# Feed-forward set-up of a two-block transformer kernel: earlier transposes, rows normed in two parts, full values on two engines, differences on VectorE

## The chip, the cores and the metric

The kernel runs on one core of a Trainium2 chip. The metric is the device time of one execution in microseconds (us), as the median of several runs; one more execution was profiled. Engines are TensorE (PE), VectorE (DVE), ScalarE (ACT), GpSimd (POOL) and SyncE (SP, which here only issues DMAs).

## What is computed

Two transformer blocks follow each other over 1024 tokens of width 1024, in float32. Each ends with a feed-forward layer; the second one's input is also scaled and shifted by a modulation vector:

```python
# first block
h = rmsnorm(x, g_mlp[l])
hid = jnp.square(jax.nn.relu(jnp.einsum("bsd,df->bsf", h, w_mlp_in[l])))   # 1024 -> 4096
x = x + jnp.einsum("bsf,fd->bsd", hid, w_mlp_out[l])                      # 4096 -> 1024
# second block
h = _modulate(_rmsnorm(x, g_ffn[l]), sh2, sc2)
a = jnp.square(jax.nn.relu(jnp.einsum('bsd,df->bsf', h, w_ff1[l])))
x = x + gt2[:, None, :] * jnp.einsum('bsf,fd->bsd', a, w_ff2[l])
```

## The kernel before

**Split values.** Each float32 operand x of a product is kept as a high part (a rounded copy, made on ScalarE) and a low part (x minus its high part, made on VectorE). One product then is three matmul passes: high by high, low by high, high by low.

**Seven products for eight.** The feed-forward layers multiply 2 x 2 blocks by a scheme with seven products, numbered p = 1 to 7. The weights come in 16 units u = 0 to 15 of 256 columns. For each unit the tokens' side `hq[p]` is the same, and the weights' side `wq[p]` is made anew. A product (p, u) has 12 matmuls of 128x512 (L2716 to L2718). The list `SEQ` gives the order: (1,0), (2,0), (5,0), (6,0), (7,0), (4,0), (3,0), (1,1), (2,1), and so on.

**The set-up.** Before the first product the tokens' operands have to be made. That is the stretch of this document, and it comes twice: k = 0 for the first block, k = 1 for the second. What stands in it:

- Ahead of it TensorE runs the output projection, in groups of 24 matmuls, a group for each block t = 0 to 7 of 128 tokens. VectorE adds each to the residual `xs` (L1924), and in the second block first multiplies it by a row (L2319, L2321). ScalarE squares and sums each row (`row_sum`, L1209), VectorE makes the reciprocal root (`norm_rstd`, L1534 to L1540, with one square root on ScalarE, L1214) and multiplies the rows into `xn` (L1898), t = 0 to 3 at once and t = 4 to 7 at once.
- TensorE transposes `xn` in 16 tiles n of four transposes each (L2694): n = 0 to 7 for tokens of the first half, 8 to 15 for the second. They go through four banks `XB`, so tile n waits until tile n - 4 has been read out.
- ScalarE reads each tile out as a full value `ft` ("hfull", L1230 or L1232). For n < 8 it also makes the high part (L1238) of `hq[1]` and `hq[2]`, and VectorE the low part (L1993).
- The operands of products 5, 6, 7 and 4 are differences of full values: for 5 and 6 made on VectorE (L2002, L2010), for 7 and 4 on GpSimd (L844, L850). Product 3 takes a full value as it is. Each gets a high part (ScalarE, L1251) and a low part (VectorE, L1993), in two pieces of 128x1024.
- ScalarE copies some finished banks aside (`part_kept`, L1261): product 7 may start only when the bank of product 6 has been copied, product 4 only when that of product 7 has. Product 3 waits for the sum that VectorE makes of product 7's bank (`hidden_added`, L1944).
- GpSimd makes sums and differences of each unit's weights (`unit_sums`). SP loads the raw weights of unit 1 after these operands are done, since `ft[0]` lies where unit 1 goes.

The engines' queues run in the order in which they are written; nothing is scheduled by a tool. The order on ScalarE in `ff_setup`, from the profiled kernel:

```python
for n in range(8):
    full(n)
    act.wait_ge(h_f.sem, h_f.base + 16 * k + n + 1)
    A_(hq[1 + n // 4][0][:, n % 4, :], ft[n // 4][:, n % 4, :], ACT.Copy).then_inc(h_hi.sem, 1)
for n in range(8, 16):
    full(n)
part_kept(k, 0, 0)
for p, i in ((5, 0), (6, 0), (7, 2), (4, 1), (3, 3)):
```

## Time and profile before

| | |
|---|---|
| median of 3 runs | 2657.48 us (2655.09 to 2666.38) |
| profiled execution, its own time | 2663.87 us |
| its span | 2662.0 us |
| TensorE, busy | 2490.0 us, 94% of the span |
| VectorE, busy | 1579.5 us, 59% |
| ScalarE, busy | 1207.3 us, 45% |
| GpSimd, busy | 858.9 us, 32% |

The span is what the profile shows of the execution; its own time is 1.9 us more. The first set-up lies at 889 to 944 us of the span, the second at 1994 to 2051 us. In the views a row of the timeline gives start, length, engine, line and operation, output <- inputs, how many were merged ("x4"), and in brackets how long the engine was idle before it and what released it.

### The profile page before, as it was taken

The page shows a single profiled execution, that of the slowest core. Times are in us where ns is not written, and L with a number is a line of the kernel's source. Part 1 is how long each engine was busy: PE and PEld are TensorE (multiplying, and loading weights), DVE is VectorE, ACT ScalarE, POOL GpSimd, SP SyncE. Part 2 cuts the span into 40 slices and gives each one's busy share as a digit, 9 for nine tenths or more (in the row PEclk, how much of TensorE's full clock was granted, in tenths as well). Part 3 has the DMA queues.
Part 4 walks back from the last instruction along what each step waited for, and adds up shares of the span by engine and source line. Part 5 has one row for each costly group of instructions (what it writes and reads, how often), then busy time and mean ns, then how long its engine had stood idle before and what let it go on. Part 6 is the DMA issues. An engine that isn't in the chain of part 4 may idle for free.

```text
span 2662.0 us, 32783 instructions
## 1 busy us (share of the span) xinstructions
PE 2490.0 (94%) x11852; PEld 2028.2 (76%) x11852; DVE 1579.5 (59%) x2792; ACT 1207.3 (45%) x2228; POOL 858.9 (32%) x756
## 2 busy tenths in 40 slices
PE   4997899999899899999999999999798999999997
PEld 3765778886677688887888887788686888878886
DVE  5347458988554587765545876334757444356676
ACT  6136446745412555554333453225426555543343
POOL 0222331221210166663242400005204565514242
PEclk9998999999999899999999998999998999999998
DMA  4102122323253156657754554423332444396354
GB/s 159 46 16 78 37 66 85 103 92 140 81 198 103 57 189 212 204 196 269 244 180 146 162 178 158 73 77 117 115 143 85 157 148 157 130 345 197 128 165 151
DMA packets 191187, 371.91 MB, mean 140 GB/s; under 512 B 13724, under 2 KB 58404, under 8 KB 190772
## 3 DMA queue, kind: packets, MB, share of 16 engines
q1 hardware_dynamic: 178676, 342.56, 39.0%
q10 hardware_dynamic: 8064, 14.68, 1.5%
q0 software_dynamic: 4288, 12.60, 1.5%
q8 instruction: 94, 1.54, 0.2%
q14 instruction: 65, 0.53, 0.1%
HBM read 269.05 MB, written 100.74 MB: 139 GB/s over the span
## 4 chain that ended last, share of the span: by engine, by line
PE 80%; DVE 7%; ACT 4%; DMA 3%; issue 3%; POOL 2%; SPq 0%; DVEq 0%; ACTq 0%; POOLq 0%
PE bank L2743 7%; PE bank L2745 7%; PE bank L2744 7%; PE bank L2716 7%; PE bank L2717 7%; PE bank L2718 7%; PE bank L2349 6%; PE bank L2350 6%; PE bank L2351 6%; PE bank L2530 3%; PE bank L2532 3%; PE bank L2531 3%; PE bank L2450 1%; DMA w_raw<-in_w_in 1%; PE bank L2439 1%
## 5 line engine op out<-in xcount | busy, mean ns | idle before, releaser
L2716 PE MATMUL bank<-hq_hi,wq_hi 128*128 128x512 f32 x896 | 352.3, 393 | 17.8 <-DVE hq_lo L1993 11.4
L2743 PE MATMUL bank<-ring_b_hi,ring_a_hi 128*128 128x512 f32 x896 | 350.5, 391 | 6.3 <-DVE hidden L1944 5.2
L2718 PE MATMUL bank<-hq_hi,wq_lo 128*128 128x512 f32 x896 | 350.8, 392 | 0.0
L2717 PE MATMUL bank<-hq_lo,wq_hi 128*128 128x512 f32 x896 | 350.6, 391 | 0.0
L2745 PE MATMUL bank<-ring_b_hi,ring_a_lo 128*128 128x512 f32 x896 | 349.9, 390 | 0.0
L2744 PE MATMUL bank<-ring_b_lo,ring_a_hi 128*128 128x512 f32 x896 | 349.8, 390 | 0.0
L2083 DVE TENSOR_TENSOR ring_a_lo<-a_raw,ring_a_hi 128x1024 fp32r<-128x1024 f32 x112 | 154.9, 1383 | 230.8 <-ACT ring_a_hi L1329 230.5
L1329 ACT ACTIVATE ring_a_hi<-a_raw 128x1024 fp32r<-128x1024 f32 x112 | 118.8, 1060 | 338.2 <-PE bank L2745 333.1
L1903 DVE TENSOR_TENSOR wq_lo<-unit_raw,wq_hi 128x512 fp32r<-128x512 f32 x160 | 162.5, 1020 | 110.3 <-ACT wq_hi L1195 107.3
L2716 PEld LDWEIGHTS bank<-hq_hi,wq_hi 128*128 128x128 f32 x896 | 169.3, 189 | 57.3 <-DVE hq_lo L1993 18.9
L2743 PEld LDWEIGHTS bank<-ring_b_hi,ring_a_hi 128*128 128x128 f32 x896 | 169.0, 189 | 42.9 <-DVE hidden L1944 6.1
L2718 PEld LDWEIGHTS bank<-hq_hi,wq_lo 128*128 128x128 f32 x896 | 169.3, 189 | 35.8
L2744 PEld LDWEIGHTS bank<-ring_b_lo,ring_a_hi 128*128 128x128 f32 x896 | 169.0, 189 | 35.3
L2745 PEld LDWEIGHTS bank<-ring_b_hi,ring_a_lo 128*128 128x128 f32 x896 | 168.9, 188 | 35.2
L2717 PEld LDWEIGHTS bank<-hq_lo,wq_hi 128*128 128x128 f32 x896 | 169.2, 189 | 34.7
L1195 ACT ACTIVATE wq_hi<-unit_raw 128x512 fp32r<-128x512 f32 x160 | 99.7, 627 | 142.6 <-PE bank L2718 99.0
L872 POOL TENSOR_TENSOR chain_b<-b_raw,chain_b 128x1024 f32<-128x1024 f32 x32 | 95.0, 2970 | 205.7 <-DMA b_raw<-in_w_ff 102.0
L777 POOL TENSOR_TENSOR w_lo<-w_raw,w_hi 128x512 fp32r<-128x512 f32 x56 | 75.4, 1355 | 258.1 <-ACT w_hi L966 253.7
L966 ACT ACTIVATE w_hi<-w_raw 128x512 fp32r<-128x512 f32 (+3 forms) x184 | 105.6, 605 | 104.1 <-DMA w_raw<-in_w_in 36.5
L2530 PE MATMUL bank<-hT_hi,w_hi 128*128 128x512 f32 x384 | 152.1, 396 | 0.1
L2532 PE MATMUL bank<-hT_hi,w_lo 128*128 128x512 f32 x384 | 150.3, 391 | 0.0
L2531 PE MATMUL bank<-hT_lo,w_hi 128*128 128x512 f32 x384 | 150.1, 391 | 0.0
(467 smaller groups left out, 5559.4 us busy)
## 6 DMA issues: line engine op xcount, KB each, us to landing
a_raw<-hidden_scratch SPq DMA_DIRECT2D x112, 512.0 KB, 3.3
hidden_scratch<-hidden SPq DMA_DIRECT2D x32, 1024.0 KB, 4.8
w_raw<-in_w_in SPq DMA_DIRECT2D x104, 256.0 KB, 2.8
hidden_scratch<-hidden SPq DMA_DIRECT2D x32, 768.0 KB, 3.6
unit_raw<-in_w_mlp_in SPq DMA_DIRECT2D x16, 1024.0 KB, 5.7
b_raw<-in_w_mlp_out SPq DMA_DIRECT2D x32, 512.0 KB, 4.5
unit_raw<-in_w_ff SPq DMA_DIRECT2D x16, 1024.0 KB, 5.4
b_raw<-in_w_ff SPq DMA_DIRECT2D x32, 512.0 KB, 4.6
```

What stands on the lines that cost most here:

```text
L1903: tt(wq[p][1][:, :, :], unit_operand(p, u), wq[p][0][:, :, :].bitcast(f32), ALU.subtract).then_inc(wq_lo.sem, 1)
L2349: mm(out, lh, rh, start=(i == 0), stop=False)
L2350: mm(out, lh, rl, start=False, stop=False)
L2530: mm(o[:, :], lh, rh, start=(k == 0), stop=False)
L2531: mm(o[:, :], lh, rl, start=False, stop=False)
L2532: l = mm(o[:, :], ll, rh, start=False, stop=(k == 7))
L2716: mm(o, lh[:, q, :], rh[:, q, :], start=(fresh and q == 0), stop=False, skip_group_check=True)
L2717: mm(o, lh[:, q, :], rl[:, q, :], start=False, stop=False, skip_group_check=True)
L2718: l = mm(o, ll[:, q, :], rh[:, q, :], start=False, stop=(q == 3), skip_group_check=True)
L2743: mm(o, ra_hi[r][:, e, js], rb_hi[r][:, e, :], start=(fresh and v == 0 and e == 0), stop=False, skip_group_check=True)
L2744: mm(o, ra_hi[r][:, e, js], rb_lo[r][:, e, :], start=False, stop=False, skip_group_check=True)
L2745: l = mm(o, ra_lo[r][:, e, js], rb_hi[r][:, e, :], start=False, stop=end, skip_group_check=True)
```

## The change

- **Transposes.** Tiles 0 to 3 are issued ahead of the last group (t = 7) of the output projection. Tiles 4 to 7 follow that group, then comes product (1,0), then tiles 8 to 15, then (2,0). The first two products wait for their low parts one by one.
- **Rows.** The second half is normed in two parts: rows t = 4 to 6 ahead of the last addition, and row 7 alone after it. ScalarE makes full values and high parts of tiles 0 to 3 between these.
- **Full values.** Of tiles 8 to 15 ScalarE makes the even ones and VectorE the odd ones.
- **Differences.** All four are made on VectorE, also those of products 7 and 4. GpSimd's first sums of unit 1 wait until the low part of product 4's operand is done.
- **Order.** Product (1,1) moves ahead of (6,0) (`MADE`), with its weights' split. The copy of product 6's bank comes ahead of the high parts of product 4.
- **Places.** `ft[0]` lies where unit 0's raw weights were, so SP loads unit 1 ahead of the set-up.

```diff
@@ -187,7 +187,7 @@
-        ft = [at(f"hfull{i}", [P, 4, HALF], f32, 8192 * i) for i in range(4)]
+        ft = [at(f"hfull{i}", [P, 4, HALF], f32, 8192 * i if i else RAW0) for i in range(4)]
...
@@ -353,7 +353,9 @@
-        AT = {v: i + 1 for i, v in enumerate(SEQ)}
+        MADE = SEQ[:3] + [(1, 1)] + [v for v in SEQ[3:] if v != (1, 1)]
+        AT = {v: i + 1 for i, v in enumerate(MADE)}
+        ROOT_AT = {j: j + (j > 1) + (j > 7) for j in range(10)}
...
@@ -382,7 +384,7 @@
-            return {1: (), 2: (), 5: (), 6: (), 7: (1, 2, 5, 6, 7)}.get(p, (p,))
+            return {1: (), 2: (), 5: (), 6: (), 7: (2, 5, 6, 7)}.get(p, (p,))
...
@@ -557,10 +559,10 @@
                 for t in range(NT):
                     sp.wait_ge(x_add, x0 + t + 1)
                     sp.dma_start(xr_d[k][:, t, :], xs[:, t, :]).then_inc(xr_out.sem, 16)
+                unit(1)
+                sp.wait_ge(wq_lo.sem, wq_lo.base + NP * k + WAT[3, 0])
                 sp.wait_ge(h_lo.sem, h_lo.base + 18 * k + 12)
                 sp.wait_ge(ht_p.sem, ht_p.base + 4 * k + 4)
-                unit(1)
-                sp.wait_ge(wq_lo.sem, wq_lo.base + NP * k + WAT[3, 0])
                 unit(2)
...
@@ -837,17 +839,7 @@
-                pool.wait_ge(h_f.sem, h_f.base + 16 * k + 16)
-                pool.wait_ge(ht_d.sem, ht_d.base + 4 * k + 2)
-                for r in range(2):
-                    j = slice(2 * r, 2 * r + 2)
-                    nc.gpsimd.tensor_tensor(ft[2][:, j, :], ft[3][:, j, :], ft[2][:, j, :], ALU.subtract).then_inc(ht_p.sem, 1)
-                pool.wait_ge(ht_d.sem, ht_d.base + 4 * k + 4)
-                pool.wait_ge(h_hi.sem, h_hi.base + 18 * k + 8)
-                pool.wait_ge(h_lo.sem, h_lo.base + 18 * k + 8)
-                for r in range(2):
-                    j = slice(2 * r, 2 * r + 2)
-                    nc.gpsimd.tensor_tensor(ft[1][:, j, :], ft[1][:, j, :], ft[0][:, j, :], ALU.subtract).then_inc(ht_p.sem, 1)
+                pool.wait_ge(h_lo.sem, h_lo.base + 18 * k + 16)
...
@@ -1208,43 +1200,61 @@
 
                 for t in range(4 * h, 4 * h + 4):
+                    if t == 7 and j in (1, 7):
+                        roots(ROOT_AT[j], 4, 7)
+                        act.wait_ge(wq_lo.sem, wq_lo.base + NP * (j // 7) + WAT[3, 0])
+                        first_tokens(j // 7, range(4))
                     act.wait_ge(*ready(t))
                     row_sum(j, t, junk)
-                roots(j, h)
+                if j in (1, 7):
+                    roots(ROOT_AT[j] + 1, 7, 8)
+                else:
+                    roots(ROOT_AT[j], 4 * h, 4 * h + 4)
...
+                for n in range(8, 16, 2):
+                    full(k, n)
                 part_kept(k, 0, 0)
                 for p, i in ((5, 0), (6, 0), (7, 2), (4, 1), (3, 3)):
+                    if p == 6:
+                        unit_hi(k, 1, 1)
+                    elif p == 4:
+                        part_kept(k, 0, 1)
                     for r in range(2):
                         if p in (5, 6):
-                            act.wait_ge(ht_d.sem, ht_d.base + 4 * k + 2 * (p - 5) + r + 1)
+                            act.wait_ge(ht_d.sem, ht_d.base + 8 * k + (r + 3 if p == 5 else r + 7))
                         elif p != 3:
                             act.wait_ge(ht_p.sem, ht_p.base + 4 * k + (0 if p == 7 else 2) + r + 1)
+                        else:
+                            act.wait_ge(ht_d.sem, ht_d.base + 8 * k + 6)
                         if p == 4 and r == 0:
                             act.wait_ge(xr_out.sem, xr_out.base + 128 * (k + 1))
                         j = slice(2 * r, 2 * r + 2)
...
@@ -1890,11 +1900,27 @@
-                norm_rstd(4 * h, 4 * h + 4, 2 + j)
+                norm_rstd(4 * h, 4 * h + 4, 2 + ROOT_AT[j])
+
+            def three_rows(j):
+
+                dve.wait_ge(n_ss, 10 + 4 * j + 3)
+                norm_rstd(4, 7, 2 + ROOT_AT[j])
+                normed_rows(4, 7)
+
+            def last_row(j):
+
+                dve.wait_ge(n_ss, 10 + 4 * j + 4)
+                norm_rstd(7, 8, 3 + ROOT_AT[j])
+                normed_rows(7, 8)
 
...
@@ -1907,6 +1933,17 @@
+
+            def hidden_lo(k, p, i, n, j, w):
+
+                dve.wait_ge(h_hi.sem, h_hi.base + 18 * k + n + 1)
+                tt(hq[p][1][:, j:j + w, :], ft[i][:, j:j + w, :], hq[p][0][:, j:j + w, :].bitcast(f32), ALU.subtract)\
+                    .then_inc(h_lo.sem, 1)
+
+            def first_tokens_lo(k, tiles):
+
+                for n in tiles:
+                    hidden_lo(k, 1 + n // 4, n // 4, n, n % 4, 1)
 
             for c in range(2):
                 if c == 0:
@@ -1919,6 +1956,9 @@
+                    if c == 1 and t == 7:
+                        three_rows(1)
+                        first_tokens_lo(0, range(3))
...
@@ -1928,8 +1968,8 @@
-            half_rstd(1, 1)
-            half_rows(1)
+            first_tokens_lo(0, range(3, 4))
+            last_row(1)
...
@@ -1988,34 +2028,54 @@
+                def difference(o, x, y, done):
+                    for r in range(2):
+                        j = slice(2 * r, 2 * r + 2)
+                        tt(ft[o][:, j, :], ft[x][:, j, :], ft[y][:, j, :], ALU.subtract).then_inc(done.sem, 1)
+
+                def low(p, i, n):
+                    for r in range(2):
+                        hidden_lo(k, p, i, n + r, 2 * r, 2)
+
+                def full(n):
+                    i, kk = n % 8, n % 4
+                    dve.wait_ge(f_tr.sem, f_tr.base + 16 * k + n + 1)
+                    o, x = ft[2 + i // 4][:, kk, :], XB[n % 4][:, :]
+                    if k:
+                        l = tsc(o, x, amod[:, 8 + i:9 + i], modc[:, 24 + i:25 + i], ALU.mult, ALU.add)
+                    else:
+                        l = tsc(o, x, cols[:, c_gmlp + i:c_gmlp + i + 1], None, ALU.mult)
+                    l.then_inc(ht_d.sem, 1)
+
+                first_tokens_lo(k, (4, 5))
+                full(9)
+                first_tokens_lo(k, (6,))
+                full(11)
+                first_tokens_lo(k, (7,))
                 dve.wait_ge(h_lo.sem, h_lo.base + 18 * k + 8)
-                dve.wait_ge(h_f.sem, h_f.base + 16 * k + 12)
-                for r in range(2):
-                    j = slice(2 * r, 2 * r + 2)
-                    tt(ft[0][:, j, :], ft[2][:, j, :], ft[0][:, j, :], ALU.subtract).then_inc(ht_d.sem, 1)
-                dve.wait_ge(ht_d.sem, ht_d.base + 4 * k + 2)
-                for r in range(2):
-                    low(5, 0, 8 + r, 2 * r, 2)
-                dve.wait_ge(h_f.sem, h_f.base + 16 * k + 16)
+                dve.wait_ge(h_f.sem, h_f.base + 12 * k + 10)
+                dve.wait_ge(ht_d.sem, ht_d.base + 8 * k + 2)
+                difference(0, 2, 0, ht_d)
+                full(13)
+                full(15)
+                dve.wait_ge(ht_d.sem, ht_d.base + 8 * k + 6)
+                low(5, 0, 8)
+                unit_lo(k, 1, 1)
+                dve.wait_ge(h_f.sem, h_f.base + 12 * k + 12)
                 dve.wait_ge(h_lo.sem, h_lo.base + 18 * k + 10)
-                for r in range(2):
-                    j = slice(2 * r, 2 * r + 2)
-                    tt(ft[0][:, j, :], ft[3][:, j, :], ft[0][:, j, :], ALU.subtract).then_inc(ht_d.sem, 1)
-                dve.wait_ge(ht_d.sem, ht_d.base + 4 * k + 4)
-                for r in range(2):
-                    low(6, 0, 10 + r, 2 * r, 2)
+                dve.wait_ge(ht_d.sem, ht_d.base + 8 * k + 6)
+                difference(0, 3, 0, ht_d)
+                dve.wait_ge(ht_d.sem, ht_d.base + 8 * k + 8)
+                low(6, 0, 10)
+                difference(2, 3, 2, ht_p)
                 dve.wait_ge(xr_out.sem, xr_out.base + 128 * (k + 1))
                 hidden_added(k, 0, T_A11)
-                for n, (p, i) in enumerate(((7, 2), (4, 1), (3, 3))):
-                    for r in range(2):
-                        low(p, i, 12 + 2 * n + r, 2 * r, 2)
+                dve.wait_ge(ht_p.sem, ht_p.base + 4 * k + 2)
+                low(7, 2, 12)
+                difference(1, 1, 0, ht_p)
+                dve.wait_ge(ht_p.sem, ht_p.base + 4 * k + 4)
+                low(4, 1, 14)
+                low(3, 3, 16)
 
             def sum_ready(k, o, j):
 
...
@@ -2605,6 +2668,19 @@
+
+            def hidden_transpose(k, x0, n):
+
+                if n % 8 == 0:
+                    pe.wait_ge(n_xn, x0 + n // 2 + 4)
+                if n in (13, 15):
+                    pe.wait_ge(ht_d.sem, ht_d.base + 8 * k + (n - 11) // 2)
+                elif n >= 4:
+                    pe.wait_ge(h_f.sem, h_f.base + 12 * k + (n - 3 if n < 12 else n // 2 + 3))
+                for j in range(4):
+                    l = nc.tensor.transpose(XB[n % 4][:, j * P:(j + 1) * P],
+                                            xn[:, n // 8 * 4 + j, (n % 8) * P:(n % 8 + 1) * P], ident[:, :])
+                l.then_inc(f_tr.sem, 1)
...
@@ -2658,6 +2734,9 @@
+                    if c == 1 and t == 7:
+                        for n in range(4):
+                            hidden_transpose(0, 10, n)
...
@@ -2685,20 +2764,14 @@
+                    hidden_transpose(k, x0, n)
                 pe.wait_ge(group_free, g1)
-                if k == 0:
-                    pe.wait_ge(h_f.sem, h_f.base + 16)
-                for m, (p, u) in enumerate(SEQ):
-                    if u == 0:
+                for m, (p, u) in enumerate(MADE):
+                    if u == 0 and p == 2:
+                        for n in range(8, 16):
+                            hidden_transpose(k, x0, n)
+                    if u == 0 and p > 2:
                         pe.wait_ge(h_lo.sem, h_lo.base + 18 * k + H_READY[p])
...
@@ -2713,6 +2786,8 @@
+                        if u == 0 and p <= 2:
+                            pe.wait_ge(h_lo.sem, h_lo.base + 18 * k + 4 * p - 3 + q)
...
```

Each engine's queue before and after, as built. VectorE in the first set-up, from the low parts of product 1 on (`hq1_lo`) to the sum on bank 3 (`hidden1`); before:

```order
L1993 TENSOR_TENSOR hq1_lo_208<-hfull0_221,hq1_hi_207 128x512 x4
L1993 TENSOR_TENSOR hq2_lo_210<-hfull1_222,hq2_hi_209 128x512 x4
L2002 TENSOR_TENSOR hfull0_221<-hfull2_223,hfull0_221 128x1024 x2
L1993 TENSOR_TENSOR hq5_lo_216<-hfull0_221,hq5_hi_215 128x1024 x2
L2010 TENSOR_TENSOR hfull0_221<-hfull3_224,hfull0_221 128x1024 x2
L1993 TENSOR_TENSOR hq6_lo_214<-hfull0_221,hq6_hi_213 128x1024 x2
L1944 TENSOR_TENSOR hidden1_226<-bank2,hidden1_226 128x512
L1993 TENSOR_TENSOR hq7_lo_218<-hfull2_223,hq7_hi_217 128x1024 x2
L1993 TENSOR_TENSOR hq4_lo_220<-hfull1_222,hq4_hi_219 128x1024 x2
L1993 TENSOR_TENSOR hq3_lo_212<-hfull3_224,hq3_hi_211 128x1024 x2
L1944 TENSOR_TENSOR hidden1_226<-bank3,hidden1_226 128x512
```

and now, from the low parts of product 2 on:

```order
L1940 TENSOR_TENSOR hq2_lo_210<-hfull1_222,hq2_hi_209 128x512 x2
L2047 TENSOR_SCALAR hfull2_223<-bank5,cols_55 128x512
L1940 TENSOR_TENSOR hq2_lo_210<-hfull1_222,hq2_hi_209 128x512
L2047 TENSOR_SCALAR hfull2_223<-bank7,cols_55 128x512
L1940 TENSOR_TENSOR hq2_lo_210<-hfull1_222,hq2_hi_209 128x512
L2034 TENSOR_TENSOR hfull0_221<-hfull2_223,hfull0_221 128x1024 x2
L2047 TENSOR_SCALAR hfull3_224<-bank5,cols_55 128x512
L2047 TENSOR_SCALAR hfull3_224<-bank7,cols_55 128x512
L1940 TENSOR_TENSOR hq5_lo_216<-hfull0_221,hq5_hi_215 128x1024 x2
L1929 TENSOR_TENSOR wq1_lo_190<-unit_raw1_206,wq1_hi_189 128x512
L2034 TENSOR_TENSOR hfull0_221<-hfull3_224,hfull0_221 128x1024 x2
L1940 TENSOR_TENSOR hq6_lo_214<-hfull0_221,hq6_hi_213 128x1024 x2
```

followed on the same queue by the operands of products 7, 4 and 3:

```order
L2034 TENSOR_TENSOR hfull2_223<-hfull3_224,hfull2_223 128x1024 x2
L1984 TENSOR_TENSOR hidden1_226<-bank2,hidden1_226 128x512
L1940 TENSOR_TENSOR hq7_lo_218<-hfull2_223,hq7_hi_217 128x1024 x2
L2034 TENSOR_TENSOR hfull1_222<-hfull1_222,hfull0_221 128x1024 x2
L1940 TENSOR_TENSOR hq4_lo_220<-hfull1_222,hq4_hi_219 128x1024 x2
L1940 TENSOR_TENSOR hq3_lo_212<-hfull3_224,hq3_hi_211 128x1024 x2
L1984 TENSOR_TENSOR hidden1_226<-bank3,hidden1_226 128x512
```

All four odd full values (`hfull2`, `hfull3` from bank5 and bank7) and the two pairs of differences for products 7 and 4 are new on this engine, and the low weights of (1,1) stand ahead of the second pair of differences.

ScalarE, from the last full values of the first half to the copy of product 7's bank; before:

```order
L1232 ACTIVATE hfull3_224<-bank6,cols_55 128x512
L1232 ACTIVATE hfull3_224<-bank7,cols_55 128x512
L1261 ACTIVATE hidden1_226<-bank0 128x512
L1251 ACTIVATE hq5_hi_215<-hfull0_221 128x1024 x2
L1251 ACTIVATE hq6_hi_213<-hfull0_221 128x1024 x2
L1251 ACTIVATE hq7_hi_217<-hfull2_223 128x1024 x2
L1251 ACTIVATE hq4_hi_219<-hfull1_222 128x1024 x2
L1251 ACTIVATE hq3_hi_211<-hfull3_224 128x1024 x2
L1261 ACTIVATE hidden1_226<-bank0 128x512
L1277 ACTIVATE hidden1_226<-hidden1_226 128x512
L1279 ACTIVATE hidden1_226<-hidden1_226 128x512
L1261 ACTIVATE hidden1_226<-bank0 128x512
```

and now:

```order
L1230 ACTIVATE hfull3_224<-bank6,cols_55 128x512
L1271 ACTIVATE hidden1_226<-bank0 128x512
L1261 ACTIVATE hq5_hi_215<-hfull0_221 128x1024 x2
L1187 ACTIVATE wq1_hi_189<-unit_raw1_206 128x512
L1261 ACTIVATE hq6_hi_213<-hfull0_221 128x1024 x2
L1261 ACTIVATE hq7_hi_217<-hfull2_223 128x1024 x2
L1271 ACTIVATE hidden1_226<-bank0 128x512
L1261 ACTIVATE hq4_hi_219<-hfull1_222 128x1024 x2
L1261 ACTIVATE hq3_hi_211<-hfull3_224 128x1024 x2
L1287 ACTIVATE hidden1_226<-hidden1_226 128x512
L1289 ACTIVATE hidden1_226<-hidden1_226 128x512
L1271 ACTIVATE hidden1_226<-bank0 128x512
```

The copy of bank 0 (product 6) has moved ahead of the high parts `hq4_hi`; the copy of product 7's bank still stands behind `hq3_hi` and the square of a hidden value.

## Rows read from the trace of the kernel before

**Rows 1.** Timeline of TensorE, first set-up: start, length, idle before and its releaser.

```profile
894.49 1.91 PE L2694 MATMUL bank<-ident,xn 128*128 128x128 f32 x16
...
919.14 0.50 PE L2716 MATMUL bank<-hq_hi,wq_hi 128*128 128x512 f32 x1 [1.52 <-DVE hq_lo L1993]
...
926.18 0.50 PE L2716 MATMUL bank<-hq_hi,wq_hi 128*128 128x512 f32 x1 [4.02 <-DVE hq_lo L1993]
...
930.16 0.63 PE L2718 MATMUL bank<-hq_hi,wq_lo 128*128 128x512 f32 x1
931.98 0.47 PE L2716 MATMUL bank<-hq_hi,wq_hi 128*128 128x512 f32 x1 [1.19 <-ACT hidden L1261]
...
935.72 0.47 PE L2716 MATMUL bank<-hq_hi,wq_hi 128*128 128x512 f32 x1 [0.78 <-ACT hidden L1261]
```

**Rows 2.** Timeline of TensorE, second set-up.

```profile
1999.40 1.91 PE L2694 MATMUL bank<-ident,xn 128*128 128x128 f32 x16
...
2025.92 0.50 PE L2716 MATMUL bank<-hq_hi,wq_hi 128*128 128x512 f32 x1 [3.37 <-DVE hq_lo L1993]
...
2042.54 0.47 PE L2716 MATMUL bank<-hq_hi,wq_hi 128*128 128x512 f32 x1 [0.78 <-ACT hidden L1261]
```

**Rows 3.** Stretches: busy (count) of PE, PEld, DVE, ACT, POOL; clock; DMA.

```profile
900.00:910.00 10.00, 8.85 (x35) 6.49 (x36) 6.42 (x11) 9.81 (x18) 0.00 (x0) 0.50 0.00 0
...
927.30:930.70 3.40, 3.40 (x9) 2.19 (x7) 3.40 (x3) 2.30 (x3) 1.07 (x1) 0.51 0.26 61
```

**Rows 4.** Timeline of VectorE, first set-up.

```profile
889.24 0.69 DVE L1924 TENSOR_TENSOR xs<-xs,bank 128x512 f32<-128x512 f32 x1 [0.41 <-PE bank L2351]
894.69 0.69 DVE L1924 TENSOR_TENSOR xs<-xs,bank 128x512 f32<-128x512 f32 x1 [4.76 <-PE bank L2351]
896.65 0.17 DVE L1534 TENSOR_SCALAR rst<-ss 128x4 f32<-128x4 f32 x1 [1.27 <-ACT junk L1209]
...
898.10 2.74 DVE L1898 TENSOR_SCALAR xn<-xs,rst 128x1024 f32<-128x1024 f32 x4
...
909.59 2.36 DVE L2002 TENSOR_TENSOR hfull<-hfull,hfull 128x1024 f32<-128x1024 f32 x2 [1.69 <-ACT hfull L1232]
916.59 2.49 DVE L1993 TENSOR_TENSOR hq_lo<-hfull,hq_hi 128x1024 fp32r<-128x1024 f32 x2 [4.63 <-ACT hq_hi L1251]
...
921.61 4.51 DVE L1993 TENSOR_TENSOR hq_lo<-hfull,hq_hi 128x1024 fp32r<-128x1024 f32 x2
```

**Rows 5.** Timeline of ScalarE, first set-up.

```profile
890.02 1.06 ACT L1209 ACTIVATE junk<-xs 128x1024 f32<-128x1024 f32 x1 [2.47 <-DVEq L1927]
...
898.42 0.67 ACT L1232 ACTIVATE hfull<-bank,cols 128x512 f32<-128x512 f32 x1
...
899.65 0.67 ACT L1232 ACTIVATE hfull<-bank,cols 128x512 f32<-128x512 f32 x1
...
907.08 4.71 ACT L1232 ACTIVATE hfull<-bank,cols 128x512 f32<-128x512 f32 x8
...
920.45 4.09 ACT L1251 ACTIVATE hq_hi<-hfull 128x1024 fp32r<-128x1024 f32 x4 [3.02 <-DVE hfull L2010]
...
931.26 0.58 ACT L1261 ACTIVATE hidden<-bank 128x512 f32<-128x512 f32 x1
...
932.39 0.64 ACT L1279 ACTIVATE hidden<-hidden 128x512 f32<-128x512 f32 x1
```

**Rows 6.** Timeline of GpSimd, first set-up.

```profile
921.63 6.74 POOL L850 TENSOR_TENSOR hfull<-hfull,hfull 128x1024 f32<-128x1024 f32 x2 [4.76 <-DVE hfull L2010]
933.88 2.39 POOL L813 TENSOR_TENSOR wsum<-unit_raw 128x512 f32<-128x512 f32 x1 [5.51 <-DMA unit_raw<-in_w_mlp_in]
...
938.20 1.62 POOL L817 TENSOR_TENSOR wsum<-unit_raw 128x512 f32<-128x512 f32 x1
```

**Rows 7.** Groups of VectorE by form: a tensor-scalar that reads PSUM, busy and mean ns.

```profile
L2119 DVE TENSOR_SCALAR bank<-bank,amod,modc 128x512 f32<-128x512 f32 x8 | 6.5, 813 | 6.3 <-PE bank L2374 6.3
```

**Rows 8.** Timeline of ScalarE, second set-up: one full value.

```profile
2004.09 0.76 ACT L1230 ACTIVATE hfull<-bank,modc,amod 128x512 f32<-128x512 f32 x1
```

77 lines of the change are left out of this document (34 added, 43 removed).

## Prediction

> **What bounds the kernel now.** TensorE does: it is busy for 2490.0 of 2662.0 us. So I read its timeline in the two set-ups first, since an engine that is busy elsewhere can gain only where it waits. In the first set-up the reader sees the last group end at 894.49, where the transposes start, and then waits ahead of products: 1.52 for (5,0) and 4.02 for (6,0), for low parts from VectorE, and 1.19 and 0.78 for (7,0) and (4,0), for copies of banks by ScalarE [rows 1]. From (4,0) at 935.72 on there is no more wait. (4,0), (3,0) and (1,1) have 36 matmuls; a matmul takes 0.227 us there, as the last group of 24 before the set-up took 5.45 us between two additions [rows 4]. So (2,1) starts at 935.72 + 8.17 = 943.9. That start is my measure, since ahead of it the same work stands in both kernels. In the second set-up it is 2042.54 + 8.17 = 2050.7 [rows 2].
>
> Second, the clock. In the stretch 900 to 910 it was granted at 0.50 (1.2 of 2.4 GHz), with transposes alone on TensorE, and at 0.51 in 927.3 to 930.7, after the 4.02 wait [rows 3]. There product (6,0) took 926.18 to about 930.6, 4.4 us, where 12 matmuls at 0.227 take 2.7: 1.7 lost [rows 1].
>
> Third, VectorE and ScalarE, for what the waits are made of [rows 4, 5], and GpSimd [rows 6]. A pair of 128x1024 low parts took 2.49 us on VectorE with GpSimd silent (at 916.59), and 4.51 beside GpSimd's subtractions (at 921.61), and those took 3.37 each.
>
> **The new chain, first set-up.** Its times are worked out from these rows, on the time scale of before; a released engine starts 0.05 to 0.2 us after its releaser, as in the rows.
>
> The last group started at 894.49 - 5.44 = 889.05. Now 16 transposes of 1.91 us [rows 1] stand ahead of it, so it ends at 896.4. They cost nothing: they stood behind it before. ScalarE ends row 6's sum at 891.2 [rows 5]. The root takes 1.45 (896.65 to 898.10) and a row 0.69 (2.74 for four) [rows 4], so three rows are normed at 894.8. ScalarE makes a full value and its high part per 1.23 us (898.42 to 899.65) [rows 5], four from 891.9 to 896.8. Three low parts of 0.62 end at 896.7, then comes the addition of t = 7, to 897.4, row 7's sum, to 898.7, its root and its row, to 900.9. That is no earlier than the 900.84 of before [rows 4]. What is new is what TensorE does meanwhile: tiles 4 to 7 and all of (1,0), done at 896.4 + 1.9 + 2.7 = 901.0.
>
> Tiles 8 to 11 follow ScalarE's full values 4 to 7, one per 1.23 from 899.4 on, to 904.3; even full values then take 0.59 (4.71 for eight) [rows 5]. The last transpose ends at about 907.1 and (2,0) at 909.8. Odd full values on VectorE have no row. Below stands an addition that reads PSUM, 0.69 [rows 4], above a tensor-scalar that reads and writes PSUM, 0.81 [rows 7]; I take 0.72, since the new one reads PSUM but writes SBUF. The ends are 0.5 us apart for four.
>
> From here VectorE sets the pace. Low part 7 ends at 905.95, the pair of differences for (5,0) at 908.3 (2.36 a pair [rows 4]), two full values at 909.75, the pair of low parts at 912.25. So (5,0) starts at 912.3. The low weights of (1,1) take 0.6, and (1,1) follows at once, to 917.75. The pair for (6,0) is made in 2.36 + 2.49: (6,0) starts at 917.8. A pair of differences, the sum on product 2's bank (0.63) and a pair of low parts make 5.5: (7,0) starts at 923.3. GpSimd is silent in all this, so I take the 2.49, not the 4.51. Differences and low parts for (4,0) end at 928.1.
>
> But (4,0) also waits for the copy of product 7's bank. On ScalarE this stands behind the second high part of (4,0), which ends at 926.7, two high parts of (3,0) at 1.02 (4.09 for four), a square in two steps, 1.25, and itself, 0.52 [rows 5]: 930.5. **(4,0) starts at 930.5**, after a wait of 4.5 us. Now GpSimd starts its sums of unit 1, at 928.2, so the two low parts of (3,0) take the contended 2.25 each: to 932.6. The sum on product 7's bank ends at 933.2, (3,0) starts at 933.3 and **(2,1) at 936.0**, against 943.9: 7.9 us earlier.
>
> A rule of the Trainium skill gives another price here. In "SBUF — State Buffer", section "Who interferes with whom", a VectorE instruction with two SBUF inputs and a GpSimd instruction that reads SBUF exclude each other, and the loser waits for the whole of the other. By it the two low parts of (3,0) would each wait for a GpSimd sum. The trace does not bear out the whole waits: the pair at 921.61 took 4.51 beside a subtraction of 3.37 [rows 4, 6], where one such wait alone would make 2.49 + 3.37 = 5.9. By the rule, two waits of 1.7 for GpSimd's sums would make 5.9 of the 4.5 in the chain, and (3,0) 1.4 later; in the forecast below that would be hidden behind (4,0). I go by the row.
>
> **The clock's share.** The 4.5 us wait ahead of (4,0) is as long as the 4.02 that cost 1.7 in (6,0) [rows 1, 3]. I charge it: (4,0) then ends at 934.9 and (3,0) starts there, 1.6 later. In the transposes of the second half the clock may also fall, as it did at 900; they then need about 2 us more, of which VectorE's chain hides more than half. I charge 0.4. Gain: 7.9 - 1.6 - 0.4 = 5.9 us.
>
> **Second set-up.** There the addition takes two instructions and a full value 0.76 instead of 0.67 [rows 8], both in both kernels: over one more instruction of 0.7, eight full values at 0.09 and four at 0.1 the new chain is 1.8 us longer, 48.8 instead of 47.0 from the group's start. That start is 1999.40 - 5.44 = 1993.96 [rows 2], so (2,1) would start at 2042.7, 8.0 earlier. Less 1.6, and less 0.7 since the slower tiles leave TensorE idler: 5.7.
>
> **What it costs elsewhere.** Four full values (2.9 us) and four differences (4.7) move to VectorE, two of them from GpSimd; they are in the chain above. Unit 1's load moves ahead of everything: SP issues it behind the eighth residual store, at about 898, and the load takes about 5.5: before, it was issued when GpSimd's last subtraction ended (921.63 + 6.74 = 928.37), and GpSimd then waited 5.51 for it [rows 6]. So it is there at about 904, and (1,1) needs its high weights only at 912. Behind ScalarE's late copy stand four weights, two squares and two weights of unit 1, then the copy of (1,1)'s bank, for which (6,1) waits. GpSimd's sums took 2.39 and then 1.7 (the third starts at 938.20 and takes 1.62 [rows 6]); from 928.2 on the last ends at about 934.1. Two more weights, the squares (2.5), two weights and the copy (0.5 each) follow: 939.3. (6,1) would start at 938.7 without the clock's loss, and at 940.3 with it. So the copy fits in the forecast with 1.0 to spare, and would be 0.6 late without the clock's loss.
>
> **Sum.** 5.9 + 5.7 = 11.6 us. The profiled execution's own 2663.87 would become 2652.3. It lies 6.4 above the median of the runs, 2657.48; against that I expect **2646**, 0.43% less. A measurement of this kernel tells a change from none at about 0.5%, 13.3 us, a time of 2644.2.
>
> **Rivals.** *The clock holds, 32%.* If the wait ahead of (4,0) costs nothing, or falls where the loss is hidden, (6,1) waits 0.6 for its copy, and the gain is 7.3 + 7.4 = 14.7: 2642.8. For it: the wait of 1.52 at 919.14 was followed by full clock, (6,0) began at full clock after its 4.02, and 1.6 of loss in (4,0) has 0.6 hidden already. Against it: each wait of 3.3 or more here was followed by a product partly at half clock.
>
> *The gain is given back, 13%.* The spare of 1.0 at (6,1) is small, and past it each us is lost in full. If all three of GpSimd's sums take 2.39, as the one at 933.88 [rows 6], and the weights' low parts on VectorE come late enough to hold GpSimd and ScalarE up once more, the copy ends at about 943: 3 us per set-up are lost, 2652. For it: three engines meet there in 10 us. Against it: in the trace before the same work ran after (7,0) with no wait on TensorE from 935.72 on.
>
> *VectorE is dearer than alone, 5%, and slower than before.* Between 906 and 928 stand 16 instructions of 128x1024 on it, priced at 1.2. If what slowed the pair at 921.61 was not GpSimd but ScalarE's high parts, they cost 2.25: 16 us later in each set-up, 8 net of the gain: 2657.5 + 16 = 2674. From 0.5 us each on no gain is left, from 0.9 on it is slower by over 0.5%. Against it: at 916.59 a pair took 2.49 right behind a high part, with ScalarE otherwise idle, so the row excludes it only in part.
>
> **Chances and range.** Forecast 50%, with a range of its own of 2644.2 to 2649. Faster by over 0.5% is the clock's rival, 0.32. Within 0.5%: forecast and given back, 0.63. Slower by over 0.5%: 0.05. The range for 8 in 10 reaches from the clock's rival with 0.69 us full values and the runs' own scatter, 2639, through the given-back case at 2652 to 2654, and leaves out the dear VectorE.
>
> **What would show it.** Right: (1,0) done ahead of tile 8; (5,0) 23.2 us after the last group's transposes began, (6,0) 5.5 behind it, (7,0) another 5.5; the wait of 4.5 at (4,0) released by ScalarE's copy; pairs at 2.4 to 2.5 on VectorE; (2,1) 47 to 49 us behind them. Wrong: odd full values over 0.81, a wait at (6,1), pairs over 3 us while GpSimd is silent, or clock losses in other places.

## The result

The changed kernel runs in 2647.5 us, median of 7 runs (2642.37 to 2650.2), against 2657.68 for the kernel before in the same comparison: ratio 0.9949, 95% interval 0.9936 to 0.9962. A second comparison gave 2643.6 against 2659.07, ratio 0.9946 (0.9932 to 0.9959). So it gains about 14 us, 0.5%. Forecast were 11.6 us and a time of 2646. The two gains lie just past the 0.5% that I had drawn as the line between faster and no change.

The profiled execution took 2647.55 us (2663.87 before). The page after:

```profile
span 2645.8 us, 32798 instructions
PE 2481.8 (94%) x11852; PEld 2024.3 (77%) x11852; DVE 1590.5 (60%) x2820; ACT 1203.4 (45%) x2222; POOL 837.6 (32%) x748
L2791 PE MATMUL bank<-hq_hi,wq_hi 128*128 128x512 f32 x896 | 352.9, 394 | 15.0 <-ACT hidden L1271 8.3
L2792 PE MATMUL bank<-hq_lo,wq_hi 128*128 128x512 f32 x896 | 350.6, 391 | 0.0
```

VectorE's busy time rose by 11.0 us and GpSimd's fell by 21.3. The product's matmuls are now L2791 to L2793; what they still wait for is ScalarE's copies.

TensorE's timeline in the first set-up, with start, length and the wait before, against [rows 1]:

```profile
887.11 1.91 PE L2681 MATMUL bank<-ident,xn 128*128 128x128 f32 x16
...
894.33 1.91 PE L2681 MATMUL bank<-ident,xn 128*128 128x128 f32 x16
...
902.67 1.97 PE L2681 MATMUL bank<-ident,xn 128*128 128x128 f32 x16 [0.58 <-ACT hfull L1230]
...
909.65 0.50 PE L2791 MATMUL bank<-hq_hi,wq_hi 128*128 128x512 f32 x1 [2.26 <-DVE hq_lo L1940]
...
920.51 0.47 PE L2791 MATMUL bank<-hq_hi,wq_hi 128*128 128x512 f32 x1 [0.78 <-ACT hidden L1271]
...
927.09 0.47 PE L2791 MATMUL bank<-hq_hi,wq_hi 128*128 128x512 f32 x1 [3.57 <-ACT hidden L1271]
...
930.13 0.63 PE L2791 MATMUL bank<-hq_hi,wq_hi 128*128 128x512 f32 x1
931.41 0.49 PE L2791 MATMUL bank<-hq_hi,wq_hi 128*128 128x512 f32 x1
...
934.25 0.39 PE L2791 MATMUL bank<-hq_hi,wq_hi 128*128 128x512 f32 x1
```

The reader sees the forecast's shape. The first 16 transposes stand ahead of the last group. (1,0) starts at 896.00 and is done ahead of tile 8. The 4.02 wait of (6,0) is gone, and the long wait is now at (4,0), for ScalarE's copy. (3,0) starts at 931.41 and (2,1) at 934.25.

The measure is the start of (2,1) from the place of the last group. That place starts at 887.11 here, with the transposes now ahead of the group, and it started at 889.05 before. The second set-up's place is 1985.97, and its (2,1) starts at 2034.65:

| start, from the place of the last group | forecast | first set-up | second set-up |
|---|---|---|---|
| (5,0) | 23.25 | 22.54 | 24.25 |
| (6,0) | 28.75 | 29.74 | 29.82 |
| (7,0) | 34.25 | 33.40 | 34.69 |
| (4,0) | 41.45 | 39.98 | 41.70 |
| (2,1), second set-up's forecast 51.1 | 48.95 | 47.14 | 48.68 |
| (2,1) before | | 54.95 | 56.86 |

The forecast for the first set-up is the prediction's, less 889.05, with its 2.0 of clock loss in the last line but one; the second's is its 48.8 with 2.3. So the gains are 7.8 and 8.2, in sum 16.0 of the 16.2 by which the span is shorter. (6,1), next behind (2,1), starts 2.72 later in both and waits for nothing.

VectorE's timeline of the first set-up, against [rows 4]:

```profile
900.21 0.75 DVE L2047 TENSOR_SCALAR hfull<-bank,cols 128x512 f32<-128x512 f32 x1
...
903.51 2.36 DVE L2034 TENSOR_TENSOR hfull<-hfull,hfull 128x1024 f32<-128x1024 f32 x2
905.79 1.41 DVE L2047 TENSOR_SCALAR hfull<-bank,cols 128x512 f32<-128x512 f32 x2
907.23 2.36 DVE L1940 TENSOR_TENSOR hq_lo<-hfull,hq_hi 128x1024 fp32r<-128x1024 f32 x2
909.51 0.68 DVE L1929 TENSOR_TENSOR wq_lo<-unit_raw,wq_hi 128x512 fp32r<-128x512 f32 x1
...
919.94 2.35 DVE L2034 TENSOR_TENSOR hfull<-hfull,hfull 128x1024 f32<-128x1024 f32 x2
922.35 5.70 DVE L1940 TENSOR_TENSOR hq_lo<-hfull,hq_hi 128x1024 fp32r<-128x1024 f32 x4
927.98 0.68 DVE L1984 TENSOR_TENSOR hidden<-bank,hidden 128x512 f32<-128x512 f32 x1
```

From 903.51 to 927.98 it has no gap of note. A pair has a length of 2.36, but the next instruction starts 2.28 after the pair's start (907.23 to 909.51). In 5.70 for four, the last pair is 5.70 - 2.28 = 3.4, not 4.5.

ScalarE and GpSimd where (4,0) waits, and where the copy for (6,1) is made:

```profile
921.19 4.08 ACT L1261 ACTIVATE hq_hi<-hfull 128x1024 fp32r<-128x1024 f32 x4 [0.82 <-DVE hfull L2034]
...
926.37 0.58 ACT L1271 ACTIVATE hidden<-bank 128x512 f32<-128x512 f32 x1
...
935.36 0.58 ACT L1271 ACTIVATE part<-bank 128x512 f32<-128x512 f32 x1
```

```profile
924.79 2.18 POOL L815 TENSOR_TENSOR wsum<-unit_raw 128x512 f32<-128x512 f32 x1 [69.12 <-DVE hq_lo L1940]
```

The copy of (1,1)'s bank ends at 935.94, and (6,1) starts at 936.97: 1.0 to spare, as the forecast had it.

Stretches of the first set-up (busy time and count of each engine, then the clock), against [rows 3]:

```profile
900.00:910.00 10.00, 6.38 (x38) 5.03 (x39) 9.36 (x12) 7.42 (x12) 0.00 (x0) 1.00 0.09 32
911.00:914.40 3.40, 3.40 (x10) 2.67 (x9) 3.34 (x4) 2.11 (x2) 0.00 (x0) 0.52 0.00 0
928.10:931.50 3.40, 3.40 (x10) 2.63 (x9) 3.20 (x3) 1.21 (x3) 3.24 (x3) 0.51 0.07 24
```

900 to 910 is at full clock now. Two pieces of 3.4 us are at 1.2 GHz: one in (5,0) and (1,1), one in (4,0), which takes 931.41 - 927.09 = 4.3 us where the next takes 2.84. In the second set-up one piece lies in the transposes of the second half instead (0.50 in 2004 to 2006), and one again in (4,0), which takes 4.24.

### The profile page after: what moved, and what is told of

It reads as the page before. It is cut to its first block, busy times and chain, and to the rows that moved or that the text cites. A ratio compares the mean times of both kernels' runs of the same rounds, so it can differ in the third digit from the quotient of the medians.

```text
span 2645.8 us, 32798 instructions
## 1 busy us (share of the span) xinstructions
PE 2481.8 (94%) x11852; PEld 2024.3 (77%) x11852; DVE 1590.5 (60%) x2820; ACT 1203.4 (45%) x2222; POOL 837.6 (32%) x748
## 4 chain that ended last, share of the span: by engine, by line
PE 56%; DVE 5%; ACT 2%; DMA 2%; POOL 1%; issue 1%; SPq 0%; DVEq 0%; ACTq 0%; POOLq 0%
PE bank L2818 7%; PE bank L2820 7%; PE bank L2819 7%; PE bank L2791 7%; PE bank L2793 7%; PE bank L2792 7%; PE bank L2412 3%; PE bank L2413 3%; PE bank L2414 3%; DMA w_raw<-in_w_in 1%; PE bank L2977 1%; DVE hfull L2034 1%; DVE ring_b_lo L2146 1%; DVE hq_lo L1940 1%; PE bank L2968 0%
## 5 line engine op out<-in xcount | busy, mean ns | idle before, releaser
L2791 PE MATMUL bank<-hq_hi,wq_hi 128*128 128x512 f32 x896 | 352.9, 394 | 15.0 <-ACT hidden L1271 8.3
L2793 PE MATMUL bank<-hq_hi,wq_lo 128*128 128x512 f32 x896 | 350.5, 391 | 0.0
L2791 PEld LDWEIGHTS bank<-hq_hi,wq_hi 128*128 128x128 f32 x896 | 169.4, 189 | 53.5 <-DVE hq_lo L1940 11.9
L2793 PEld LDWEIGHTS bank<-hq_hi,wq_lo 128*128 128x128 f32 x896 | 169.3, 189 | 35.7
```

The lines of the kernel that those rows point to most:

```text
L2791: mm(o, lh[:, q, :], rh[:, q, :], start=(fresh and q == 0), stop=False, skip_group_check=True)
L2793: l = mm(o, ll[:, q, :], rh[:, q, :], start=False, stop=(q == 3), skip_group_check=True)
```

## The experiments

All are compared by the start of (6,1) from the last group's place, since some of them add a wait there. Ratios are to the kernel before, with 95% intervals. Beside (1,1) behind (3,0), GpSimd's sums early, the first run of the filled gap and product 7's copy early, the kernel before had a median of 2659.05; beside the other parts undone 2658.43; beside the repeats, the early rows alone and the last kernel 2659.07.

| kernel | median us | ratio | (6,1), first | (6,1), second |
|---|---|---|---|---|
| before | 2657.68 | | 57.67 | 59.58 |
| changed kernel | 2647.5 | 0.9949 (0.9936 to 0.9962) | 49.86 | 51.40 |
| the same again | 2643.6 | 0.9946 (0.9932 to 0.9959) | 49.88 | 51.38 |
| no early rows or transposes | 2652.14 | 0.9976 (0.9966 to 0.9986) | 54.79 | 55.33 |
| two differences on GpSimd | 2649.01 | 0.9970 (0.9957 to 0.9982) | 54.68 | 54.46 |
| copy of product 6's bank late | 2649.66 | 0.9969 (0.9960 to 0.9979) | 53.02 | 54.47 |
| (1,1) behind (3,0) | 2649.36 | 0.9966 (0.9955 to 0.9976) | 51.99 | 53.89 |
| full values all on ScalarE | 2649.08 | 0.9947 (0.9931 to 0.9963) | 51.67 | 52.74 |
| early rows and transposes alone | 2654.87 | 0.9980 (0.9969 to 0.9990) | 55.88 | 57.57 |
| GpSimd's sums early | 2649.10 | 0.9970 (0.9960 to 0.9980) | 52.91 | 56.31 |
| gap ahead of (4,0) filled | 2638.66 | 0.9929 (0.9909 to 0.9949) | 49.00 | 50.89 |
| the same again | 2642.3 | 0.9938 (0.9925 to 0.9952) | 49.45 | 50.87 |
| product 7's copy early | 2641.88 | 0.9937 (0.9915 to 0.9959) | 50.75 | 50.51 |
| copies early, two gaps filled | 2640.57 | 0.9933 (0.9920 to 0.9946) | 47.93 | 50.33 |

The two right-hand columns come from one profiled execution each. In the changed kernel's two they agree within 0.02 us, in the filled kernel's within 0.45. By the intervals of the ratios alone, only the kernel without early rows and transposes, and the one with them alone, are clear of the changed kernel in both its comparisons; for the other parts the cost rests on the profiles.

**The changed kernel again.** No edit.

> The changed kernel once more, in the same batch as three others, for a closer figure of what it gains. Its profiled execution was 16.2 us shorter than that of before, and 15.9 of it lies in the two set-ups, while the first comparison gave a ratio of 0.9949 and medians 10.2 us apart. Theory: the set-ups are worth about 16 us less about 2 by chance in the clock elsewhere, ratio 0.994 to 0.996. Rival: part of the gain is given back where the profile did not show it, ratio 0.997 or nearer to 1.

The set-ups came out within 0.03 us of the first profile, and the ratio was 0.9946. Nothing shows that the set-ups' gain is given back later; the interval still leaves room for about 5 us.

### One part undone

**No early rows or transposes.** The second half is normed after the last addition and all transposes follow the last group; the rest is as changed.

```diff
-                    if c == 1 and t == 7:
-                        for n in range(4):
-                            hidden_transpose(0, 10, n)
...
-                for n in range(4, 8):
+                for n in range(8):
                     hidden_transpose(k, x0, n)
```

> The changed kernel without the early transposes and without the norm in two parts: eight tiles follow row 7, as before the change. My chain: the rows are complete at the same time, but ScalarE and VectorE then have four tiles more to do behind them, 4 x 1.23 = 4.9 us on ScalarE; (5,0) and all after it, (2,1) too, 3.5 to 4.5 us later in each set-up, 7 to 9 us in all. Rival (the rows' end sets it, so the early tiles hide nothing): within 1 us.

Undone, it costs 4.9 and 3.9 us, the first more than expected: (4,0) also took 5.08 there, against 4.32. This is the largest part by the sum of both.

**Two differences on GpSimd.** Those of products 7 and 4 go back; GpSimd's sums still wait for the low parts of (4,0).

```diff
+                    nc.gpsimd.tensor_tensor(ft[2][:, j, :], ft[3][:, j, :], ft[2][:, j, :], ALU.subtract).then_inc(ht_p.sem, 1)
...
+                    nc.gpsimd.tensor_tensor(ft[1][:, j, :], ft[1][:, j, :], ft[0][:, j, :], ALU.subtract).then_inc(ht_p.sem, 1)
...
-                difference(2, 3, 2, ht_p)
...
-                difference(1, 1, 0, ht_p)
```

> The changed kernel with the differences of products 7 and 4 back on GpSimd. My theory (GpSimd's reads slow VectorE, not ScalarE's copies): VectorE saves 4.7 us of its own, but its pairs beside GpSimd take 4 to 4.6 us instead of 2.3, and low part of (4,0) ends 1 to 4 us later; (2,1) 1 to 3 us later in each set-up, 2 to 6 us in all. Rival (VectorE is the pace, so any work off it helps): pairs stay at 2.3, (2,1) 2 to 4 us earlier.

It costs 4.8 and 3.1 us, more than expected. VectorE and GpSimd in its first set-up:

```profile
905.82 4.50 DVE L1951 TENSOR_TENSOR hq_lo<-hfull,hq_hi 128x1024 fp32r<-128x1024 f32 x2
910.25 2.85 DVE L1940 TENSOR_TENSOR wq_lo<-unit_raw,wq_hi 128x512 fp32r<-128x512 f32 x1
...
915.42 4.56 DVE L1951 TENSOR_TENSOR hq_lo<-hfull,hq_hi 128x1024 fp32r<-128x1024 f32 x2
...
920.50 3.94 DVE L1951 TENSOR_TENSOR hq_lo<-hfull,hq_hi 128x1024 fp32r<-128x1024 f32 x2
```

```profile
905.93 6.61 POOL L846 TENSOR_TENSOR hfull<-hfull,hfull 128x1024 f32<-128x1024 f32 x2 [51.65 <-DVE hfull L2058]
915.44 6.79 POOL L852 TENSOR_TENSOR hfull<-hfull,hfull 128x1024 f32<-128x1024 f32 x2 [2.90 <-DVE hfull L2045]
```

VectorE has two pairs fewer, which saves it 4.6 us. But the three pairs of low parts beside GpSimd take 4.50, 4.56 and 3.94 instead of 2.36 each, and the low weights of (1,1) 2.85 instead of 0.68: 8.1 us more. So GpSimd costs VectorE more than it takes off it, and (7,0) and (4,0) depend on its 6.6 and 6.8 us besides.

The rows also show what one such wait is. The first two subtractions end at 909.24 and 912.54. The low weights stand listed from 910.25 to 913.09, so they end 0.55 behind the second subtraction: they waited until it was done.

**Copy of product 6's bank late.** It goes back behind all high parts.

```diff
-                    elif p == 4:
-                        part_kept(k, 0, 1)
...
-                    elif p == 6 and u:
+                    elif p == 6:
                         part_kept(k, u, 1)
```

> The changed kernel with one part undone: the copy of product 6's bank is back behind the high parts of (4,0) and (3,0). My chain: (7,0) then starts after that copy, about 5.3 us later than in the changed kernel, with a wait of about 6 us on ScalarE; the copy of product 7's bank follows, so (4,0) starts 2.3 us later, and (2,1) 0.5 to 2.3 later (47.1 and 48.7 us after the slot of the last group become 47.6 to 51). Rival (the order of copies does nothing, since (4,0) waits for ScalarE anyway): (2,1) within 0.5 us. Whole kernel: 1 to 5 us slower than the changed one by my chain, 0 by the rival.

TensorE in its first set-up; the edit moves a ScalarE copy, and this row names VectorE:

```profile
921.50 0.76 PE L2789 MATMUL bank<-hq_hi,wq_hi 128*128 128x512 f32 x1 [7.77 <-DVE hq_lo L1938]
927.38 0.47 PE L2789 MATMUL bank<-hq_hi,wq_hi 128*128 128x512 f32 x1 [0.78 <-ACT hidden L1269]
```

```profile
920.78 0.57 ACT L1269 ACTIVATE hidden<-bank 128x512 f32<-128x512 f32 x1
```

(7,0) waits 7.77 us instead of 0.78. The copy ends at 921.35 and (7,0) starts at 921.50, while its low parts had been ready since 915.6. So the wait ends with the copy, though the row puts it down to VectorE; in the second set-up the same wait, 6.18, is put down to ScalarE's copy. (4,0) then waits 0.78 instead of 3.57, and 3.2 and 3.1 us are the net cost, where 0.5 to 2.3 were expected. The half-clock loss moves with the long wait: here it is in (7,0), which takes 927.38 - 921.50 - 0.78 = 5.1 us.

**(1,1) behind (3,0).** The order of before, and its weights' split with it.

```diff
-        MADE = SEQ[:3] + [(1, 1)] + [v for v in SEQ[3:] if v != (1, 1)]
+        MADE = list(SEQ)
...
-                    if p == 6:
-                        unit_hi(k, 1, 1)
...
-                unit_lo(k, 1, 1)
```

> The changed kernel with product (1,1) back in its old place behind (3,0), its weights' split with it. My chain: nothing fills the time between (5,0) and (6,0), which VectorE sets; (6,0), (7,0) and (4,0) start 0.6 us earlier (low weights gone from VectorE), the 2.7 us of (1,1) come at the end: (2,1) 2.1 us later, up to 3.7 if the longer wait lowers the clock. 4 to 7 us in all. Rival (the order costs nothing as ScalarE and VectorE are the pace to the end): within 0.5 us.

It costs 2.1 and 2.5 us. TensorE then waits in four places of the first set-up, 2.24, 1.82, 2.12 and 2.47; in the changed kernel it is three, 2.26, 0.78 and 3.57, so (1,1) fills 2.0 us of waits, as work that depends on nothing late. No wait here is longer than 2.5 us, and yet (4,0), behind the last of four, took 4.28 and 4.25 us at a mean clock of 0.63. So the half-clock loss doesn't need a wait of 3.6 us or more; several shorter ones in a row brought it too.

**Full values all on ScalarE.**

```diff
-                for n in range(8, 16, 2):
+                for n in range(8, 16):
                     full(k, n)
...
-                full(9)
...
-                full(11)
...
-                full(13)
-                full(15)
...
```

> The changed kernel with all full values back on ScalarE. My chain: ScalarE ends them 1.9 us later, so the high part of (5,0) and with it VectorE's low parts start about 1.1 us later, although VectorE has 2.9 us less to do; (5,0) to (4,0) and (2,1) 0.5 to 1.5 us later, 1 to 3 us in all. Rival (VectorE alone is the pace): (5,0) about 1 to 2 us earlier, 2 to 4 us faster in all.

By the set-ups it costs 1.8 and 1.3 us. The runs don't show it: four are 2641.6, 2642.73, 2649.08 and 2659.27. A fifth, of 14068 us, is an outlier that the table's median, 2649.08, counts and the ratio does not; without it the median is 2645.9. The profiled one has a span of 2657.5 with a mean clock of 0.975. The difference in span to the changed kernel's, 11.7, is mostly not in the set-ups; the last section comes back to it.

The undone parts add up to 16.8 and 13.9 us, where the whole change brings 7.8 and 8.2. So the parts don't add. A likely reason is that the set-up is one chain through three engines, where any part taken out can become the slowest piece. The next run shows it for one part; the others were not tried by themselves.

**Early rows and transposes alone.** The kernel before with that part, with (1,0) ahead of tiles 8 to 15, and with unit 1's load ahead. No other part.

> Of the change only the early part: three rows normed ahead, four tiles transposed ahead of the last group, (1,0) ahead of tiles 8 to 15, and unit 1's load ahead. Full values on ScalarE, two pairs of differences on GpSimd, (1,1) behind (3,0) and the copies in their old places. Undoing this part alone cost 4.9 and 3.9 us. Theory that the parts cover one another (one chain over three engines, where the slowest piece left decides): alone it brings less than that, about 2.8 us, (2,1) 52 us from the group's start instead of 55.0, ratio 0.998. Rival, that the parts add: 4.9 and 3.9 us, (2,1) at 50 and 53, ratio 0.9965.

It brings 1.8 and 2.0 us, where undoing the same part cost 4.9 and 3.9. About 2.8 were expected. VectorE shows where the rest of the gain went:

```profile
908.69 5.30 DVE L1944 TENSOR_TENSOR hq_lo<-hfull,hq_hi 128x1024 fp32r<-128x1024 f32 x2 [1.61 <-ACT hq_hi L1265]
...
921.58 11.72 DVE L1944 TENSOR_TENSOR hq_lo<-hfull,hq_hi 128x1024 fp32r<-128x1024 f32 x6
```

(7,0) was still 3.4 us earlier than before (39.54 against 42.93 from the place). But GpSimd's subtractions lie beside two pairs again, and with unit 1 loaded early its sums start at 923.26 and lie beside the last ones: six low parts take 11.72, 1.95 each, against 8.48 in the kernel before. So part of the loss here is the early load's and not the rows'. How much of it reached TensorE, I can't tell from this run; no run has the early load alone.

### The prices in dispute

**GpSimd's sums early.** They wait for the low parts of (5,0) instead of those of (4,0).

```diff
-                pool.wait_ge(h_lo.sem, h_lo.base + 18 * k + 16)
+                pool.wait_ge(h_lo.sem, h_lo.base + 18 * k + 10)
```

> The changed kernel with GpSimd's first sums of unit 1 let go once the low part of (5,0) is done, not that of (4,0). Theory (GpSimd's reads slow VectorE): three sums of about 2.2 us run beside the differences and low parts of (6,0) and (7,0); a pair there takes 3.5 to 4.6 us instead of 2.3, (6,0) starts about 2 to 3 us later, (2,1) 1 to 2.5 later: 2 to 5 us slower in all. Rival (what slows VectorE is ScalarE): pairs stay at 2.3, (6,0) in place, and with the weights ready earlier (2,1) is up to 1 us earlier.

```profile
908.75 4.53 DVE L2034 TENSOR_TENSOR hfull<-hfull,hfull 128x1024 f32<-128x1024 f32 x2
913.32 3.34 DVE L1940 TENSOR_TENSOR hq_lo<-hfull,hq_hi 128x1024 fp32r<-128x1024 f32 x2
916.59 2.35 DVE L2034 TENSOR_TENSOR hfull<-hfull,hfull 128x1024 f32<-128x1024 f32 x2
```

```profile
908.32 1.66 POOL L815 TENSOR_TENSOR wsum<-unit_raw 128x512 f32<-128x512 f32 x1 [53.99 <-DVE hq_lo L1940]
910.06 2.15 POOL L817 TENSOR_TENSOR unit_raw<-unit_raw 128x512 f32<-128x512 f32 x1
912.28 2.16 POOL L819 TENSOR_TENSOR wsum<-unit_raw 128x512 f32<-128x512 f32 x1
```

The first set-up is 3.0 longer, the second 4.9, where 1 to 2.5 each were expected; in the second (4,0) and (3,0) also took 5.25 and 3.20, at a mean clock of 0.64. Three sums of 6.0 us in all make two VectorE pairs 3.2 us longer, 2.2 and 1.0. The same pair takes 2.35 as soon as GpSimd is silent. So 1.2 for a VectorE instruction alone was right, and the difference comes from GpSimd. ScalarE's high parts ran beside VectorE's cheap pairs in every one of these traces, and the rival "VectorE is dearer than alone" falls with that.

The Trainium skill has a rule for this, in "SBUF — State Buffer", section "Who interferes with whom": the two engines exclude each other and the loser waits for the whole of the other's instruction. The trace agrees. The sums end at 909.98, 912.21 and 914.44, and a VectorE instruction ends 1.1 behind each, at 911.06, 913.29 and 915.53; 1.1 is the distance of two such instructions when VectorE is alone. The three waits cost 3.2 and not 6.0 because the listed lengths of the sums hold their own waits for VectorE: a sum beside an idle VectorE takes 1.3 (933.16 to 934.46 in this run), the later two of these 2.15. It is the same with GpSimd's subtractions in the kernel before. In turn with VectorE they took 3.37 each [rows 6], and beside a VectorE idle until 916.59 they took 2.4 each:

```profile
912.10 4.77 POOL L844 TENSOR_TENSOR hfull<-hfull,hfull 128x1024 f32<-128x1024 f32 x2 [54.49 <-DVE hfull L2002]
```

**The gap ahead of (4,0) filled.** Twelve matmuls on ready tiles, into a bank that nobody reads.

```diff
+                    if (p, u) == (4, 0):
+                        pe.wait_ge(wq_lo.sem, wq_lo.base + NP * k + WAT[4, 0])
+                        for q in range(12):
+                            mm(XB[3][:, :], wq[4][0][:, q % 4, :], hq[7][0][:, q % 4, :], start=(q == 0), stop=(q == 11),
+                               skip_group_check=True)
```

> The changed kernel with 12 added matmuls (their result is never read) between (7,0) and (4,0), 2.7 us in a wait of 3.6 and 4.0. Theory (the wait lowers the clock): no 0.5 clock at (4,0), its 12 matmuls take 2.7 to 3.0 instead of 4.2, (2,1) 1.2 to 1.6 us earlier in each set-up; of that up to 0.5 is lost again at (6,1), whose bank copy comes then. 1.5 to 3 us faster in all. Rival (the clock's fall is not from this wait): (4,0) still takes 4.2 and nothing is gained, or the added work comes in the way and costs up to 1 us.

```profile
921.89 2.88 PE L2777 MATMUL bank<-hq_hi,wq_hi 128*128 128x512 f32 x12
926.01 0.47 PE L2796 MATMUL bank<-hq_hi,wq_hi 128*128 128x512 f32 x1 [1.24 <-ACT hidden L1271]
...
928.82 0.39 PE L2796 MATMUL bank<-hq_hi,wq_hi 128*128 128x512 f32 x1
...
935.02 0.47 PE L2796 MATMUL bank<-hq_hi,wq_hi 128*128 128x512 f32 x1 [0.61 <-ACT part L1271]
```

The stretch of (4,0) in this kernel, and one that is mostly (3,0):

```profile
926.00:929.50 3.50, 3.49 (x16) 2.91 (x17) 3.35 (x4) 1.02 (x2) 3.42 (x2) 1.00 0.34 129
928.10:931.50 3.40, 3.40 (x16) 2.81 (x15) 3.10 (x3) 2.27 (x4) 3.24 (x3) 1.00 0.00 0
```

(4,0) starts at the same distance from the place, 39.99 against 39.98, and takes 2.81 us at full clock instead of 4.32. The first wait after (4,0) is then at (6,1), 0.61 us, for the copy of (1,1)'s bank: what the forecast's first rival said, and of its size in the first set-up (0.93 in the second). Net of it 0.9 and 0.5 us are kept. The ratio was 0.0020, or 5 us, below the changed kernel's, which the set-ups do not explain. The same kernel again:

> The twelve idle-time matmuls ahead of (4,0) once more (they multiply ready tiles into a bank that nobody reads; the sums are as before). By the first trace the product (4,0) then runs at full clock and (2,1) starts 1.6 us earlier in each set-up, of which (6,1) keeps 0.9 and 0.5, since it then waits for the copy of (1,1)'s bank. Theory: it is worth about 1.4 us against the changed kernel, and the 5 us by which the first comparison had it faster was chance in the clock elsewhere. Rival: the full clock carries on beyond the set-up, and it is worth 4 to 6 us.

Beside the changed kernel it was 1.3 us faster by the medians, 0.4 and 0.5 by the set-ups, with intervals that overlap. The rest of the first figure did not come again, so I take it for scatter.

### Towards a better version

**Product 7's copy early.** Ahead of the high parts of (3,0), with the sum on that bank ahead of the low parts of (3,0).

```diff
+                    elif p == 3:
+                        part_kept(k, 0, 2)
...
                 low(4, 1, 14)
+                hidden_added(k, 0, T_A22)
                 low(3, 3, 16)
```

> The changed kernel with the copy of product 7's bank ahead of the high parts of (3,0) on ScalarE, and the sum on that bank ahead of the low parts of (3,0) on VectorE. My chain: (4,0) starts 2.4 us earlier, when its low part is done, (3,0) and (2,1) 3.3 us earlier; but (6,1) then waits about 2.3 us for the copy of (1,1)'s bank, which ends as late as before, so about 1 us is kept in each set-up: 2 us faster in all. Rival (no other wait behind it): 3.3 us kept in each, 6.6 in all.

```profile
927.61 0.47 PE L2794 MATMUL bank<-hq_hi,wq_hi 128*128 128x512 f32 x1 [0.78 <-ACT hidden L1273]
932.95 0.80 PE L2794 MATMUL bank<-hq_hi,wq_hi 128*128 128x512 f32 x1 [2.35 <-DVE hq_lo L1942]
```

```profile
928.45 4.44 DVE L1942 TENSOR_TENSOR hq_lo<-hfull,hq_hi 128x1024 fp32r<-128x1024 f32 x2 [0.19 <-ACT hq_hi L1263]
```

(4,0) starts 1.5 earlier from the place (38.43), but (3,0) now waits 2.35, for low parts that start later and both lie beside GpSimd's sums, 4.44 for the pair. Behind that wait (3,0) took 4.26 us. In the first set-up this loses 0.9 and in the second it gains 0.9, where 1 us kept in each was expected: the wait, and in the first set-up the clock's loss, went from one product to the next. The median, 2641.88 of 4 runs, is no evidence for more.

**Copies early, two gaps filled.** In addition the copy of (1,1)'s bank goes directly behind the high parts of (2,1), and 8 and 6 idle matmuls stand ahead of (4,0) and (3,0).

```diff
                             unit_hi(k, p_, u + 1)
+                            if (p_, u) == (2, 0):
+                                act.wait_ge(h_lo.sem, h_lo.base + 18 * k + 18)
+                                part_kept(k, 1, 0)
...
+                    if u == 0 and p in (4, 3):
+                        pe.wait_ge(wq_lo.sem, wq_lo.base + NP * k + WAT[p, 0])
+                        for q in range(8 if p == 4 else 6):
+                            mm(XB[3][:, :], wq[p][0][:, q % 4, :], hq[7][0][:, q % 4, :], start=(q == 0),
+                               stop=(q == (7 if p == 4 else 5)), skip_group_check=True)
```

> Copy of product 7's bank ahead of the high parts of (3,0), the copy of (1,1)'s bank behind the high parts of (2,1), and idle-time matmuls in the gaps: 8 ahead of (4,0), 6 ahead of (3,0). With the early copy alone (4,0) started 38.4 and 39.5 us from the group's start instead of 40.0 and 41.7, (3,0) waited 2.35 and 1.67 for its low parts, and part of (3,0) was at half clock. Theory: with the gaps filled (2,1) starts at 46.5 and 46.0 instead of 47.1 and 48.7, (6,1) at 49.3 and 48.8 instead of 49.9 and 51.4, so about 3 us less than the changed kernel, and half-clock periods in the set-ups are fewer. Rival: VectorE has become the bound there, and the filled gaps only move the waits: no gain over the changed kernel.

```profile
900.00:935.00 35.00, 29.29 (x136) 23.09 (x136) 33.61 (x32) 23.81 (x35) 8.43 (x5) 1.00 0.17 55
```

The first set-up is at full clock, and VectorE is busy for 33.61 of these 35 us. The second is not: 2000 to 2012 has 0.86. (6,1) starts 1.9 and 1.1 earlier than in the changed kernel, 3.0 in sum as expected, though the expectation had 0.6 and 2.6. The medians of the same comparison are 3.0 apart. The intervals of the two ratios overlap. So this version has the shortest set-ups and the lowest median of its comparison, but the runs alone don't show it to be the fastest; the filled kernel's first median, in another comparison, was 2638.66.

## Why the prediction was right, and where it was off

- **Early transposes, three rows, (1,0) ahead of tile 8.** As forecast, to the order: low part 7 ended at 903.5, 16.4 us from the place, forecast 16.9. The run without early rows and transposes puts 4.9 and 3.9 us on these. (1,0) stayed ahead of tile 8 in it, and no run moved it back.
- **VectorE sets the pace.** Right, and its odd full values took 0.746 and, in the second set-up, 0.806 each, inside the bounds of 0.69 and 0.81. **The term that was mis-sized is the pair.** I took 2.36 and 2.49, the listed lengths in [rows 4]. What counts on a busy engine is the distance of starts, 2.28. Seven pairs stand ahead of the differences' end for (4,0): 16.0 us instead of 16.9. With the 0.5 ahead of them that is the 1.5 us by which (4,0) came earlier than forecast. It is most of the 1.8 and 2.4 us by which each set-up beat its sum; 0.5 more of the second's is its clock charge, below.
- **The contended pair of (3,0), and the rule that I set aside.** Charged 4.5, it took 3.4. It was hidden behind (4,0) either way. The 2.25 for each low part was an average over a pair that did not behave evenly, and the reading behind it was wrong. At 921.61 in the kernel before, the first low part took 1.23 as if alone, and the second was listed at 3.37 and ended at 926.12, 1.08 behind the end of GpSimd's first subtraction. That is one wait for a whole subtraction. I held 2.49 + 3.37 = 5.9 against it, but the subtraction's 3.4 holds its own wait for VectorE. Beside an idle VectorE a subtraction takes 2.4, as shown under the early sums. So the row agrees with the rule of the Trainium skill ("SBUF — State Buffer", section "Who interferes with whom"). It is chance that 2.25 was also right beside sums: there each low part waits 1.1, in the pair of 921.61 one of two waits 2.2. In the changed kernel the first low part of (3,0) began at 924.63, ahead of the sum, and only the second waited: 1.14 + 2.29 = 3.4.
- **The clock.** The 1.6 charged to (4,0) was right: 4.32 us against the 2.81 of the filled kernel, 1.5 lost. That a wait of the 3.6 to 4 us kind costs this was the choice between the forecast and its first rival, and the filled gap shows it from the other side. The further 0.4 and 0.7 were expected in the transposes. In the first set-up of the first profile the loss sat in (5,0) and (1,1) instead, 911.0 to 914.4. They took 4.05 and 3.15 where 2.72 each is full clock, which is 1.8 us. In the second it did sit in the transposes, and (2,0) started at 19.98 from the place, against 18.74 in the repeat. Little of either got through, since VectorE sets the pace. In the repeat's first set-up (5,0) and (1,1) ran at full clock, and (7,0) started at 33.20 instead of 33.40. In its second (4,0) started at 41.52 instead of 41.70. So each of them was worth about 0.2. And as a sign for this loss the length of a single wait was too simple: with (1,1) behind (3,0) a wait of 2.5, the last of four, was followed by it too.
- **The spare at (6,1).** Forecast 1.0 us, measured 1.0. The rival in which the gain is given back there did not come. It is small all the same: the filled kernel ran into it in both set-ups, and the one with product 7's copy early in the second, by 0.55.
- **GpSimd silent until (4,0)'s operands are made.** Needed: letting its sums in early cost 3.0 and 4.9 us.
- **The sum.** 16.0 instead of 11.6 in the profile, about 14 by the ratios of two comparisons. The rest between 16 and 14 is inside the intervals. The mechanism was the forecast's, with the wait and the loss at (4,0), but the size lies nearer the 14.7 of its first rival. That the first median, 2647.5, came within 1.5 us of the forecast's 2646 is partly luck: the gain in the set-ups was 4.4 larger than the sum, and that median lay above the repeat's 2643.6 for the same set-ups.

## What to carry to other kernels

Cost a chain on a busy engine from start to start, not by the listed lengths, which overlap. Taking half of a job off the bounding engine is no help if the helper makes the other half wait: measure the pair beside the helper, and read listed lengths with care, since those of both engines hold their waits for each other. And when several edits shorten one chain, undoing each and adding up overstates the whole (16.8 for 7.8 here), while one of them alone can bring little (1.8 for the one that was tried); look for the wait that appears next, and for independent work, like (1,1), to put into it.

## What the runs showed of the hardware

**Idle matmuls keep the clock.** Twelve matmuls in the gap of about 4 us ahead of (4,0) brought the following product from 4.32 to 2.81 us, though they cost TensorE 2.88 us of its own.

**VectorE and GpSimd take turns by whole instructions.** With two inputs in SBUF on VectorE, and GpSimd reading SBUF too, each instruction waited, where they met in these rows, until the other engine's was done. So a GpSimd sum is listed at 1.3 us alone and at 2.15 in turn with VectorE, and a subtraction at 2.4 and 3.4; VectorE's 1.2 becomes 2.3 behind a sum and 3.4 behind a subtraction. VectorE's addition of a bank, with one input in PSUM, kept its 0.68 beside a subtraction (919.90, with two differences on GpSimd).

**The same code ahead of the change starts at scattered times.** The place of the last group lies at 889.05 in the kernel before and at 887.11, 882.41 and 890.29 in the changed kernel, its repeat, and the one with all full values on ScalarE. The instructions ahead of it are in the same order in all four. Part of it is seen in the attention stage, first of the changed kernel, then of the one with all full values on ScalarE:

```profile
240.00:330.00 90.00, 64.14 (x423) 52.43 (x422) 46.08 (x179) 40.97 (x133) 30.17 (x69) 0.91 0.20 61
```

```profile
240.00:330.00 90.00, 64.81 (x406) 52.06 (x403) 43.54 (x172) 40.63 (x130) 27.69 (x60) 0.85 0.18 58
```

With a clock of 0.85 instead of 0.91, 406 matmuls instead of 423 were done in the same 90 us. The clock isn't all of it: the repeat of the changed kernel did 434 matmuls there, also at 0.91, and its place came 4.7 us earlier with the very same kernel. So executions differ by as much as the effects studied here. It is why the set-ups were measured from their own start. What makes the clock fall in one execution and not in another stayed open.
